# Modulation loads issued by SP, twelve weight low parts made on GpSimd, and four loads moved behind the stream

## The chip, the cores and the metric

The kernel runs on one core of one Trainium2 chip. The metric is the device time of one execution in microseconds, the median of several runs.

## The reference

Two transformer blocks in float32 on x of 1024 tokens by 1024 features, one after the other:

```
first_block:  x += hgrn2_mixer(rms(x)) ;  x += relu(rms(x) @ w1)^2 @ w2 ;  x = rms(x) * norm_final
second_block: sh1, sc1, g1, sh2, sc2, g2 = silu(c) @ w_ada + b_ada       (the same for the context, from c_ctx)
              hc = rms(ctx) * norm1 * (1 + csc1) + csh1                  (256 context tokens)
              hx = rms(x) * norm1 * (1 + sc1) + sh1
              kc, vc = hc @ w_in ;  fx, q, k, v = hx @ w_in
              y_four = real(fft2(fx)) ;  y_attn = windowed attention over k, v and kc, vc
              x += g1 * ((gate_f * (y_four @ w_fo) + gate_a * (y_attn @ w_ao)) @ w_o)
              x += g2 * relu((rms(x) * norm2 * (1 + sc2) + sh2) @ w1)^2 @ w2
```

Both hidden layers of the MLPs have 4096 features. silu(c) @ w_ada is a "modulation": 48 tiles for c and the first 16 of them for the context, each a product of a 128 x 1024 tile with a row, summed along the row.

## The kernel before, in words

**Precision.** Each float32 product is made of three TensorE products of rounded parts: `hi*hi`, `lo*hi`, `hi*lo`. ScalarE makes a high part (`Whi`, `Ah`, `Bh`, `ftr_h`, `wgt_h`, `Hh`) by a copy that rounds, VectorE the low part (`Wlo`, `Al`, ...) by a subtraction. Some low parts are made on GpSimd.

**Programs.** The five engines each run a program written by hand, one function for each (`tensor_program`, `sync_program`, `scalar_program`, `vector_program`, `gpsimd_program`). Each waits on semaphores by name, and its order is the order in the text. SP issues nearly all DMAs and stands when a DMA's condition isn't met; everything behind it in its program stands too.

**Weights.** Apart from those of the MLPs, weights come as a list `WT` of 128 x 1024 tiles of 512 KB. SP loads tile n into `Wraw[n % 2]` when tile n-2 has both its parts; ScalarE makes `Whi[n % 4]` and VectorE `Wlo[n % 4]` (line 1999) when TensorE has done with tile n-4. Every engine calls `feed(to)` at points in its program to go on to that tile. `S2_0[0]` is the number of the first tile of the second block. The tiles from there are, two each: ctx_v0, ctx_v1, ctx_k0, ctx_k1, u0, u1; then four of the Fourier matrix (dft), then others.

**An MLP** (`mlp(0)` and `mlp(1)`; the second is that of the second block) is done by a fast block scheme with seven products x = 1..7 of sums and differences of blocks.
- *Product stage*: 112 products s of 12 matmuls. They go through `SEQ`, by groups q of seven: 1, 5, then 4 of group q-1, 6, then 3 of q-1, 2, 7. For each group SP loads `pair_raw[q % 2]` (two DMAs of 512 KB, `pair_load`). VectorE makes sums of its pieces (`a_sum`, lines 2188 to 2200) four products ahead and low parts `Al` (`a_part`, line 2208) three ahead. VectorE scales and adds the results (`quarter`), ScalarE squares them, VectorE makes four sums of them (`feature_sums`), and SP writes three quarters and four sums of each group to `b_scratch` (256 KB each, at most three under way; `quarter_out`, `sums_out`).
- *Stream stage*: 56 steps g of 24 matmuls, 8 for each x in the order 1, 5, 6, 2, 7, 3, 4. SP's `step_load(j, g)` brings weights (`wgt_r`, for x = 5 and 7 also `other`) and features (`ftr_r`) when TensorE has done with the step that had the place (six before) and ScalarE is done with step g-4. `step_split` makes the four parts. In `mlp(0)` the last three steps of x = 4 go feature tile by feature tile (line 932).

**The modulations** are done on VectorE beside `mlp(0)`: `modulation(u)`, u = 0..97. It multiplies a 128 x 1024 tile `mraw` with `cvec` (line 2328) or, for u from 66 on, a tile of the second MLP's weights with the shift row (line 2332), and sums along it. u = 0 and u = 49 make the silu of `c` and `c_ctx` in `cvec`. Up to u = 48 they stand in the product stage, at every second product. The others stand in the stream by the table `MODS`: one in steps 4 to 7, 16, 17, 26 and on, two in steps 18 to 25. GpSimd's program issues the load of u (`mraw`, two buffers) as soon as modulation u-2 is done.

**Around the stream's end.** The final norm of the first block adds up squares in `facc`, on ScalarE (`final_square`), VectorE and GpSimd (`final_add`, lines 2341 and 2753), in steps 37 to 55. The context's squares are added in steps 41 to 43. In steps 49 and 53 ScalarE and VectorE call `feed` for the first four tiles, SP does at 44 and 51:

```
for g in range(7, 56):
    ...
    step_load(j, g)
    if j == 0:
        if g in (44, 51):
            sp.wait_ge(S("w_sum").at(39))
            feed(S2_0[0] + (2 if g == 44 else 4))
```

The tiles' places lie in memory that the stream's `wgt_s` and `other` hold until late. After the stream come: the root of the context norm, the context operand (`hcT`, `hch`, `hcl`), the last four final squares, the roots of the final norm for each half of the tokens, `HT` = the normed x of the second block (line 2440), `Hh` on ScalarE (line 1724), `Hl` on VectorE (line 2445). TensorE does ctx_v0, a sum, ctx_v1, ctx_k0, ctx_k1, then `u0` and `u1` from `Hh` and `Hl`, then dft.

Of the kernel before, what the change touches and what calls it, by code (L numbers as in the profile page):

```python
# [91 lines left out]
def build(nc, xT, vecs, w_in, w_out, m_w1, m_w2, ctxT, c_d, w_ada, w_in2, gains, biasE, biasM, w_gate, w_fo, w_ao,  # L92
          w_o2, m2_w1, m2_w1T, m2_w2, ident_d, masks_d, rope_d, dft_d, cd_d, out):
    with ExitStack() as ctx:
# [162 lines left out]
        S2_0 = [len(WT)]  # L257
        for c0 in (1536, 1792, 1024, 1280, 0, 256):
            WT += [cols256(w_in2, c0, 0), cols256(w_in2, c0, 512)]
        WT += [dft_d[par, cs].rearrange("(k p) c -> p k c", p=P) for par in range(2) for cs in range(2)]  # L260
# [49 lines left out]
        S = Sems()  # L310
# [197 lines left out]


        def tensor_program(pe):  # L510
# [19 lines left out]
            def lo_of(n):  # L530
                return S("w_lo", "v").at(n)
# [641 lines left out]
        def sync_program(sp):  # L1173
# [88 lines left out]
            def stream_loads(j):  # L1262
# [9 lines left out]
                if j == 0:  # L1272
                    e.dma_start(gnq[:], gains).then_inc(*S("gains").tick(0, 16))
                for g in range(7, 56):
# [7 lines left out]
                    if j == 0:  # L1282
                        if g in (44, 51):
                            sp.wait_ge(S("w_sum").at(39))
                            feed(S2_0[0] + (2 if g == 44 else 4))
                        if g == 24:
                            e.dma_start(cx[:], ctxT.rearrange("k p t -> p k t")).then_inc(*S("cx").tick(0, 16))
                    elif g in (42, 50):
                        result_out(2 if g == 42 else 7)
                if j:  # L1290
                    result_out(3)
                    result_out(4)

# [7 lines left out]
            def first_stage(j):  # L1301
# [102 lines left out]
        def scalar_program(act):  # L1404
# [322 lines left out]
            for g in range(4, 56):  # L1727
# [8 lines left out]
                if g in (49, 53):  # L1736
                    feed(S2_0[0] + (2 if g == 49 else 4))
# [6 lines left out]

            rstd("ctx_norm", 4, crs, 256)
# [243 lines left out]
        def vector_program(dve):  # L1989
# [3 lines left out]
            def feed(to):  # L1993
                for n in range(fed[0], to):
                    dve.wait_ge(S("w_hi").at(n))
# [347 lines left out]
            def beside(g):  # L2343
# [8 lines left out]
                if g in (49, 53):  # L2352
                    feed(S2_0[0] + (2 if g == 49 else 4))
# [93 lines left out]

            dve.wait_ge(stream_full(0, 52))
# [11 lines left out]
            for k in range(8):  # L2460
                h2_normed(k, 1)
                if k == 4:
                    feed(upto(("ctx_v0", 1)))
            mean_square(0)
            both_roots(0)
            feed(upto(("ctx_v1", 1)))
            for k in range(10):
                if k < 8:
                    h2_normed(k, 0)
                if k >= 2:  # L2470
                    h2_lo(k - 2)
                if k == 8:
                    feed(upto(("ctx_k0", 1)))
            feed(upto(("ctx_k1", 1)))
# [210 lines left out]
        def gpsimd_program(pool):  # L2685
            e = pool.e

# [43 lines left out]
            def modulation(u):  # L2731

                w, j = (0, u - 1) if u < 49 else (1, u - 50)
                if j < 0:
                    pool.wait_ge(S("ada").at(u - 1) if u else full_at(("mlp_norm", 0), 1))
                    e.dma_start(cvec[:], c_d[w]).then_inc(*S("c").tick(w, 16))
                    return
                if u in (1, 2):
                    pool.wait_ge(S("xs_out").at(0), S("lo", "v").at(b_lo(0, 3, 3)))
                elif u in (50, 51):  # L2740
                    pool.wait_ge(S("c_scaled").at(63))
                if u % 49 >= 2:
                    pool.wait_ge(S("ada").at(u - 2))
                e.dma_start(mod_place(u)[:], w_ada[j] if u < 66 else m2_w1T[u - 66]).then_inc(
                    *S("ada_raw", u % 2).tick(u, 16))

# [8 lines left out]
            for u in range(52):  # L2755
                modulation(u)
            for g in range(4, 56):
                for u in MODS.get(g, ()):
                    if u >= 52:
                        modulation(u)  # L2760
                if FINAL_AT.get(g, 11) not in (0, 4, 11):
                    final_add(FINAL_AT[g])
                for k in CTX_AT.get(g, ()):
                    if not 1 <= k < 7:
                        continue
                    pool.wait_ge(sq_of(4).at((4, k, 0, 0)))
                    if k > 1:
                        pool.wait_ge(sum_of(4).at((4, k - 1)))
                    e.tensor_tensor(cacc[:], cacc[:], csq[:], ALU.add).then_inc(*sum_of(4).tick((4, k)))
# [121 lines left out]
```

## Time and profile before

| | |
|---|---|
| median of 3 runs | 2678.27 us (2677.73 to 2681.16) |
| the profiled execution | 2677.73 us, its span 2675.9 us |
| TensorE (PE) busy | 2593.2 us, 97% of the span |
| VectorE (DVE) | 1743.1 us, 65% |
| ScalarE (ACT) | 1180.9 us, 44% |
| GpSimd (POOL) | 208.1 us, 8% |
| product stage of mlp(0) | about 600 to 928 us |
| stream stage of mlp(0) | about 928 to 1253 us |

The span goes from the first to the last instruction. Engines overlap, so their shares don't add up. In timelines and groups a row names line, engine, operation and output<-input; what stands in square brackets is how long the engine had been idle before it and what released it. SPq and POOLq are the issues of DMAs. A matmul's busy time overlaps its neighbours', so the distance of their starts is what one takes.

### The profile page before, as it was taken

To read this page: it belongs to the slowest core of one execution; us is meant where nothing else is said; L and a number is where in the kernel's file an instruction comes from. 1 tells how busy PE (TensorE), PEld (TensorE's weight loads), DVE (VectorE), ACT (ScalarE), POOL (GpSimd) and SP (SyncE) were. 2 spreads that over 40 slices of the span, in tenths; PEclk is the share of its full clock that TensorE was granted. 3 is DMA by queue.
4 is the path that set the end of the run, shared out by engine and by line. 5 is a ranking of instruction groups with operands and counts; after the bars stand their busy time and mean duration, and the time that the engine had idled before them with its cause. 6 is when DMAs were issued, how large, how long until landed. Compare 5 with 4: busy or idle time off the path is not lost.

```text
span 2675.9 us, 41694 instructions
## 1 busy us (share of the span) xinstructions
PE 2593.2 (97%) x16880; PEld 2162.6 (81%) x16880; DVE 1743.1 (65%) x2471; ACT 1180.9 (44%) x1852; POOL 208.1 (8%) x245
## 2 busy tenths in 40 slices
PE   8999999899999999999899999999899999999999
PEld 7887878687777787787889878977777888888887
DVE  6445454568888877897634565566566777768573
ACT  5454453544343443356333344244444555554341
POOL 2222122300000001132000000000000000000000
PEclk9999999999999999999999999999999999999999
DMA  4101111234776899983423212121352354488664
GB/s 138 41 25 48 36 30 41 80 110 154 235 230 215 282 375 328 338 294 127 145 85 120 69 57 78 33 70 57 132 207 95 121 167 139 164 313 290 236 224 140
DMA packets 289744, 406.12 MB, mean 152 GB/s; under 512 B 14736, under 2 KB 161680, under 8 KB 289552
## 3 DMA queue, kind: packets, MB, share of 16 engines
q1 hardware_dynamic: 275440, 352.07, 38.8%
q0 software_dynamic: 14112, 51.39, 5.7%
q8 instruction: 134, 2.20, 0.3%
q14 instruction: 58, 0.48, 0.1%
HBM read 314.27 MB, written 89.13 MB: 151 GB/s over the span
## 4 chain that ended last, share of the span: by engine, by line
PE 55%; DVE 12%; DMA 8%; issue 3%; ACT 3%; SPq 1%; DVEq 0%; ACTq 0%
PE ps L917 13%; PE ps L845 4%; PE ps L847 4%; PE ps L849 4%; DMA b_scratch<-qb 3%; PE ps L1101 2%; PE ps L1102 2%; PE ps L1106 2%; PE ps L567 2%; PE ps L551 2%; PE ps L554 2%; PE ps L635 2%; PE ps L633 2%; PE ps L637 2%; DVE Al L2208 1%
## 5 line engine op out<-in xcount | busy, mean ns | idle before, releaser
L847 PE MATMUL ps<-Bh,Al 128*128 128x512 f32 x896 | 352.4, 393 | 15.5 <-DVE Al L2208 15.5
L845 PE MATMUL ps<-Bh,Ah 128*128 128x512 f32 x896 | 351.5, 392 | 5.3 <-ACT wb L1598 3.9
L1999 DVE TENSOR_TENSOR Wlo<-Wraw,Whi 128x1024 fp32r<-128x1024 f32 x100 | 123.1, 1245 | 246.7 <-ACT Whi L1420 246.6
L849 PE MATMUL ps<-Bl,Ah 128*128 128x512 f32 x640 | 249.3, 389 | 0.0
L633 PE MATMUL ps<-Whi,Hh 128*128 128x256 f32 x768 | 222.4, 290 | 5.1 <-issue 5.1
L1620 ACT ACTIVATE ftr_h<-ftr_r 128x1024 fp32r<-128x1024 f32 x112 | 118.5, 1058 | 240.3 <-DMA ftr_r<-b_scratch 240.3
L635 PE MATMUL ps<-Wlo,Hh 128*128 128x256 f32 x768 | 217.9, 284 | 1.2 <-DVE Wlo L1999 1.2
L637 PE MATMUL ps<-Whi,Hl 128*128 128x256 f32 x768 | 217.6, 283 | 0.0
L917 PE MATMUL ps<-ftr_l,wgt_h 128*128 128x512 f32 x848 | 210.0, 390 | 5.3 <-DVE ftr_l L2276 5.3
L847 PEld LDWEIGHTS ps<-Bh,Al 128*128 128x128 f32 x896 | 169.2, 189 | 56.3 <-DVE Al L2208 21.1
L917 PE MATMUL ps<-ftr_h,wgt_h 128*128 128x512 f32 x848 | 210.1, 390 | 0.0
L917 PE MATMUL ps<-ftr_h,wgt_l 128*128 128x512 f32 x848 | 209.6, 389 | 0.0
L845 PEld LDWEIGHTS ps<-Bh,Ah 128*128 128x128 f32 x896 | 169.3, 189 | 42.8 <-ACT wb L1598 4.7
L1420 ACT ACTIVATE Whi<-Wraw 128x1024 fp32r<-128x1024 f32 x100 | 103.6, 1053 | 227.1 <-PE ps L567 92.0
L917 PEld LDWEIGHTS ps<-ftr_l,wgt_h 128*128 128x128 f32 x848 | 158.8, 188 | 39.8 <-DVE ftr_l L2276 6.9
L917 PEld LDWEIGHTS ps<-ftr_h,wgt_h 128*128 128x128 f32 x848 | 159.2, 188 | 33.5 <-issue 0.5
L917 PEld LDWEIGHTS ps<-ftr_h,wgt_l 128*128 128x128 f32 x848 | 159.1, 188 | 33.3 <-DVE wgt_l L2282 0.3
L2276 DVE TENSOR_TENSOR ftr_l<-ftr_r,ftr_h 128x1024 fp32r<-128x1024 f32 x112 | 136.9, 1222 | 28.3 <-ACT ftr_h L1620 28.2
L633 PEld LDWEIGHTS ps<-Whi,Hh 128*128 128x128 f32 x768 | 147.6, 192 | 7.1 <-issue 5.6
L635 PEld LDWEIGHTS ps<-Wlo,Hh 128*128 128x128 f32 x768 | 147.7, 192 | 1.6 <-DVE Wlo L1999 1.5
L637 PEld LDWEIGHTS ps<-Whi,Hl 128*128 128x128 f32 x768 | 147.7, 192 | 0.0
L849 PEld LDWEIGHTS ps<-Bl,Ah 128*128 128x128 f32 x640 | 120.3, 188 | 25.0
(372 smaller groups left out, 5471.0 us busy)
## 6 DMA issues: line engine op xcount, KB each, us to landing
b_scratch<-qb SPq DMA_DIRECT2D x224, 256.0 KB, 4.4
wgt_r<-in_m_w SPq DMA_DIRECT2D x112, 512.0 KB, 4.9
ftr_r<-b_scratch SPq DMA_DIRECT2D x112, 512.0 KB, 6.2
pair<-in_m_w SPq DMA_DIRECT2D x64, 512.0 KB, 5.3
mraw<-in_w_ada POOLq DMA_DIRECT2D x64, 512.0 KB, 5.5
Wraw<-in_w_in SPq DMA_DIRECT2D x56, 512.0 KB, 4.1
other<-in_m_w SPq DMA_DIRECT2D x32, 512.0 KB, 6.0
mraw<-in_m_w1T POOLq DMA_DIRECT2D x32, 512.0 KB, 5.4
```

What stands on the lines that cost most here:

```text
L551: e.matmul(t[:, c], wh[:, k, ms], opd.hi[:, k, c], start=k == 0, stop=False)
L633: e.matmul(o, opd.hi[:, k, c], wh[:, k % 4, :], start=k == 0, stop=False)
L635: e.matmul(o, opd.hi[:, k, c], wl[:, k % 4, :], start=False, stop=False)
L637: i = e.matmul(o, opd.lo[:, k, c], wh[:, k % 4, :], start=False, stop=k == 7)
L845: e.matmul(o, h[:, k, :], Bh[x][:, k, :], start=first and k == 0, stop=False, skip_group_check=not first)
L847: e.matmul(o, l[:, k, :], Bh[x][:, k, :], start=False, stop=False, skip_group_check=not first)
L849: i = e.matmul(o, h[:, k, :], Bl[x][:, k, :], start=False, stop=k == 3, skip_group_check=not first)
L917: ins = e.matmul(o(m), a, b, start=not cont and g == 8 * i and n == 0 and k == 0, stop=last, skip_group_check=cont)
L1420: e.activation(Whi[n % 4][:], Wraw[n % 2][:], ACT.Copy).then_inc(*S("w_hi").tick(n))
L1620: e.activation(ftr_h[p][:], ftr_r[p][:], ACT.Copy).then_inc(*S("a_hi").tick(2 * G))
L1999: e.tensor_tensor(Wlo[n % 4][:], Wraw[n % 2][:], Whi[n % 4][:].bitcast(F), ALU.subtract).then_inc(*S("w_lo", "v").tick(n))
L2276: e.tensor_tensor(ftr_l[p][:], ftr_r[p][:], ftr_h[p][:].bitcast(F), ALU.subtract).then_inc(*S("a_lo").tick(2 * G))
```

## The change

- SP's program issues the loads of the modulations; they leave GpSimd's program. In the product stage they stand behind products 6, 8, 9 and then every odd one. In the stream, u = 49, 50 and 51 stand in front of step 7's load, and those of `MODS[g - 1]` behind the load of step g.
- The load of a `pair` stands one product later in SP's program, behind the sums and a quarter of the product before: at product 4 of group q for group q+2. Before, it stood in front of them, at product 5.
- The first four tiles of the second block are no longer fed within the stream, on SP, ScalarE or VectorE, but behind it.
- `Wlo` of twelve tiles, from the fifth on (ctx_k0, ctx_k1, u0, u1, dft), is made by GpSimd. VectorE's `feed` skips them, and its calls for them in between `HT` and `Hl` go. TensorE and SP wait on GpSimd's semaphore for them.
- GpSimd's additions keep their order, without the loads between them.

```diff
+        LO_POOL = [len(WT) + 4, 0]
         for c0 in (1536, 1792, 1024, 1280, 0, 256):
             WT += [cols256(w_in2, c0, 0), cols256(w_in2, c0, 512)]
+        LO_POOL[1] = len(WT) + 4
...
         sync_program, feed:
-                        sp.wait_ge(S("w_hi").at(n - 2), S("w_lo", "v").at(n - 2))
+                        sp.wait_ge(S("w_hi").at(n - 2), S("w_lo", "p" if on_pool(n - 2) else "v").at(n - 2))
...
         stream_loads:
                 if j == 0:
+                    for u in (49, 50, 51):
+                        modulation(u)
                     e.dma_start(gnq[:], gains).then_inc(*S("gains").tick(0, 16))
                 for g in range(7, 56):
                     ...
                     step_load(j, g)
                     if j == 0:
-                        if g in (44, 51):
-                            sp.wait_ge(S("w_sum").at(39))
-                            feed(S2_0[0] + (2 if g == 44 else 4))
+                        for u in MODS.get(g - 1, ()):
+                            if u >= 52:
+                                modulation(u)
...
         first_stage:
-                    if x == 5 and 1 <= q % 16 < 15:
-                        pair_load(q + 1)
+                    if x == 4 and q % 16 < 14:
+                        pair_load(q + 2)
                     if s % NS >= 3:
                         if SEQ[s - 3][0] == 2 and SEQ[s - 3][1] % 16:
                             sums_out(SEQ[s - 3][1] - 1)
                         quarter_out(s - 3)
                     if s % NS in (107, 108, 111):
                         step_load(j, (107, 108, 111).index(s % NS))
+                    if s in (6, 8, 9):
+                        modulation((6, 8, 9).index(s))
+                    elif s < NS and s >= 11 and s % 2 and (s - 5) // 2 < 49:
+                        modulation((s - 5) // 2)
                 stream_loads(j)
             first_stage(0)
+            sp.wait_ge(S("w_sum").at(39))
+            feed(S2_0[0] + 2)
...
         scalar_program and vector_program, in the steps:
-                if g in (49, 53):
-                    feed(S2_0[0] + (2 if g == 49 else 4))
         behind the steps, ahead of the context root and norm:
+            feed(S2_0[0] + 4)
...
         vector_program:
             for k in range(8):
                 h2_normed(k, 1)
-                if k == 4:
-                    feed(upto(("ctx_v0", 1)))
             mean_square(0)
             both_roots(0)
-            feed(upto(("ctx_v1", 1)))
             for k in range(10):
                 if k < 8:
                     h2_normed(k, 0)
                 if k >= 2:
                     h2_lo(k - 2)
-                if k == 8:
-                    feed(upto(("ctx_k0", 1)))
-            feed(upto(("ctx_k1", 1)))
...
         gpsimd_program:
+            def feed(to):
+                for n in range(fed[0], to):
+                    if not on_pool(n):
+                        continue
+                    pool.wait_ge(S("w_hi").at(n), weight_full(n - 4))
+                    e.tensor_tensor(Wlo[n % 4][:], Wraw[n % 2][:], Whi[n % 4][:].bitcast(F), ALU.subtract).then_inc(
+                        *S("w_lo", "p").tick(n))
+                fed[0] = max(fed[0], to)
...
             norm_lo(HC, hcT, True, 256)
             for n in range(12, 15):
                 final_add(n)
+            for name in ("ctx_v0", "ctx_v1", "ctx_k0", "ctx_k1", "u0", "u1"):
+                feed(upto((name, 1)))
             pool.wait_ge(S("xs").at(7))
```

The function `modulation` of the GpSimd program goes to SP's as it is, its waits too: the load of u waits for modulation u-2.

## Rows read from the trace of the kernel before

**Rows 1.** TensorE's waits, whole span: us in total, times, longest.

```profile
PE ps L847 <- DVE Al L2208: 15.5, 11, 2.6
...
PE ps L917 <- DVE ftr_l L2276: 5.3, 3, 2.5
```

**Rows 2.** VectorE's waits in the product stage, 600 to 920.

```profile
DVE Xs L2188 <- DMA pair<-in_m_w: 34.8, 14, 4.5
```

**Rows 3.** VectorE's waits in the stream stage, 930 to 1240.

```profile
DVE mraw L2332 <- DMA mraw<-in_m_w1T: 10.2, 4, 2.9
DVE mraw L2328 <- DMA mraw<-in_w_ada: 8.3, 6, 2.0
```

**Rows 4.** Windows: busy us (instructions) of each engine, clock, DMA share, GB/s.

```profile
928.00:1000.00 72.00, 72.00 (x316) 58.91 (x315) 53.69 (x62) 31.98 (x32) 2.63 (x5) 1.00 1.01 374
1000.00:1100.00 100.00, 94.70 (x415) 77.39 (x414) 80.31 (x97) 33.68 (x33) 11.62 (x22) 1.00 0.93 329
1100.00:1150.00 50.00, 50.00 (x222) 41.40 (x221) 48.70 (x60) 21.23 (x23) 8.98 (x11) 1.00 0.98 361
...
1990.00:2676.00 686.00, 679.72 (x2982) 560.43 (x2981) 465.85 (x589) 318.58 (x448) 0.00 (x0) 1.00 0.55 186
```

**Rows 5.** Timeline of SP's queue: start, us, engine, line, what.

```profile
945.74 0.51 SPq L1273 DMA_DIRECT2D gnq<-in_gains  x1
...
1189.63 0.37 SPq L1256 DMA_DIRECT2D wgt_r<-in_m_w  x1
...
1205.75 1.50 SPq L1182 DMA_DIRECT2D Wraw<-in_w_in  x2
1207.35 0.64 SPq L1256 DMA_DIRECT2D wgt_r<-in_m_w  x1
```

**Rows 6.** Timeline of VectorE, 1180 to 1420.

```profile
1204.46 2.35 DVE L1999 TENSOR_TENSOR Wlo<-Wraw,Whi 128x1024 fp32r<-128x1024 f32 x2
...
1217.54 1.22 DVE L2276 TENSOR_TENSOR ftr_l<-ftr_r,ftr_h 128x1024 fp32r<-128x1024 f32 x1 [1.50 <-ACT ftr_h L1620]
...
1225.07 3.32 DVE L1999 TENSOR_TENSOR Wlo<-Wraw,Whi 128x1024 fp32r<-128x1024 f32 x2
...
1231.19 1.77 DVE L2341 TENSOR_TENSOR facc<-facc,ftmp 128x512 f32<-128x512 f32 x1
...
1254.40 3.95 DVE L2440 SCALAR_TENSOR_TENSOR HT<-R,modA,rs 128x512 f32<-128x512 f32 x5
1260.32 2.36 DVE L1999 TENSOR_TENSOR Wlo<-Wraw,Whi 128x1024 fp32r<-128x1024 f32 x2 [1.97 <-ACT Whi L1420]
```

**Rows 7.** Timeline of TensorE around the start of ctx_v0 and of u0.

```profile
1253.21 0.28 PE L633 MATMUL ps<-Whi,hch 128*128 128x256 f32 x1
1253.33 0.28 PE L635 MATMUL ps<-Wlo,hch 128*128 128x256 f32 x1
...
1284.95 0.55 PE L633 MATMUL ps<-Whi,Hh 128*128 128x256 f32 x1 [5.12 <-issue]
1286.73 0.58 PE L635 MATMUL ps<-Wlo,Hh 128*128 128x256 f32 x1 [1.23 <-DVE Wlo L1999]
```

**Rows 8.** Timeline of ScalarE, 1180 to 1420.

```profile
1234.31 1.28 ACT L1412 ACT_TABLE_LOAD   x1
```

**Rows 9.** The page's costliest groups: busy, mean ns, idle before.

```profile
L1999 DVE TENSOR_TENSOR Wlo<-Wraw,Whi 128x1024 fp32r<-128x1024 f32 x100 | 123.1, 1245 | 246.7 <-ACT Whi L1420 246.6
...
L1420 ACT ACTIVATE Whi<-Wraw 128x1024 fp32r<-128x1024 f32 x100 | 103.6, 1053 | 227.1 <-PE ps L567 92.0
```

**Rows 10.** DMA issues: count, KB each, median us to landing.

```profile
mraw<-in_w_ada POOLq DMA_DIRECT2D x64, 512.0 KB, 5.5
Wraw<-in_w_in SPq DMA_DIRECT2D x56, 512.0 KB, 4.1
```

**Rows 11.** GpSimd by shape, whole span; then its timeline.

```profile
L2727 POOL TENSOR_TENSOR Hl<-R,Hh 128x1024 fp32r<-128x1024 f32 x4 | 10.0, 2492 | 21.6 <-ACT Hh L1564 21.6
...
1224.17 2.01 POOL L2753 TENSOR_TENSOR facc<-facc,ftmp 128x512 f32<-128x512 f32 x1 [3.11 <-ACT ftmp L1699]
```

More of the change, by code:

```diff
@@ L507, in upto, with on_pool @@
             return min(WN[name] + 5, len(WT))
+        def on_pool(n):
+            return LO_POOL[0] <= n < LO_POOL[1]
         def tensor_program(pe):
@@ L530, in lo_of @@
             def lo_of(n):
-                return S("w_lo", "v").at(n)
+                return S("w_lo", "p" if LO_POOL[0] <= n < LO_POOL[1] else "v").at(n)
             def empty(b, occ):
@@ L1292, in stream_loads, with modulation @@
                     result_out(4)
+            def modulation(u):
+                w, j = (0, u - 1) if u < 49 else (1, u - 50)
+                if j < 0:
+                    sp.wait_ge(S("ada").at(u - 1) if u else full_at(("mlp_norm", 0), 1))
+                    e.dma_start(cvec[:], c_d[w]).then_inc(*S("c").tick(w, 16))
+                    return
+                if u in (1, 2):
+                    sp.wait_ge(S("xs_out").at(0), S("lo", "v").at(b_lo(0, 3, 3)))
+                elif u in (50, 51):
+                    sp.wait_ge(S("c_scaled").at(63))
+                if u % 49 >= 2:
+                    sp.wait_ge(S("ada").at(u - 2))
+                e.dma_start(mod_place(u)[:], w_ada[j] if u < 66 else m2_w1T[u - 66]).then_inc(
+                    *S("ada_raw", u % 2).tick(u, 16))
             def result_out(x):
@@ L1994, in feed @@
                 for n in range(fed[0], to):
+                    if on_pool(n):
+                        continue
                     dve.wait_ge(S("w_hi").at(n))
@@ L2351, in beside @@
                     modulation(u)
-                if g in (49, 53):
-                    feed(S2_0[0] + (2 if g == 49 else 4))
                 if g == 30:
@@ L2446, in h2_lo @@
                                        ALU.subtract).then_inc(*S("lo", "v").tick((5, k, 0)))
+            feed(S2_0[0] + 4)
             dve.wait_ge(stream_full(0, 52))
@@ L2686, in gpsimd_program @@
             e = pool.e
+            fed = [0]
+            def feed(to):
+                for n in range(fed[0], to):
+                    if not on_pool(n):
+                        continue
+                    pool.wait_ge(S("w_hi").at(n), weight_full(n - 4))
+                    e.tensor_tensor(Wlo[n % 4][:], Wraw[n % 2][:], Whi[n % 4][:].bitcast(F), ALU.subtract).then_inc(
+                        *S("w_lo", "p").tick(n))
+                fed[0] = max(fed[0], to)
             def norm_lo(opd, Tk, shifted=False, n=T):
@@ L2728, in gpsimd_program @@
                         *S("lo", "p").tick((2, h, 0)))
[L2731 to L2745, printed above, removed]
             def final_add(n):
@@ L2753, in final_add @@
                 e.tensor_tensor(to, to, ftmp[1][:], ALU.add).then_inc(*sum_of(5, 1).tick((5, n)))
[L2755 to L2769, printed above, removed]
+            for n in range(1, 4):
+                final_add(n)
+            for k in range(1, 7):
+                pool.wait_ge(sq_of(4).at((4, k, 0, 0)))
+                if k > 1:
+                    pool.wait_ge(sum_of(4).at((4, k - 1)))
+                e.tensor_tensor(cacc[:], cacc[:], csq[:], ALU.add).then_inc(*sum_of(4).tick((4, k)))
+            for n in range(5, 11):
+                final_add(n)
             norm_lo(HC, hcT, True, 256)
```

## The prediction

> **What bounds the kernel now.** I read the page first, then the windows of the stretch that the edits touch, then who waited for whom on TensorE and VectorE there, and last the timelines of SP, VectorE, ScalarE and GpSimd around the end of the first MLP. TensorE is the engine that sets the time nearly everywhere, so an edit counts only where it changes one of TensorE's waits. Of those waits the edits can reach five places. (a) In the product stage of the first MLP (about 600 to 928 us) TensorE waited 15.5 us for VectorE's low parts of the weight pieces [rows 1]; VectorE itself waited there 34.8 us, 14 times, for the `pair` loads [rows 2]. (b) In the stream stage it waited 5.3 us for `ftr_l` [rows 1]. VectorE was late there because it waited 18.5 us (10.2 + 8.3, ten waits) for the `mraw` loads of the modulations [rows 3], while the DMA engines were 0.93 to 1.01 occupied [rows 4]. (c) The last four steps of the stream: SP issued step 51's load at 1189.63, then stood before the `Wraw` loads until 1205.75, and the load of step 52 went out only at 1207.35 [rows 5]. (d) After the stream everything up to the `u0` product hangs on a chain of small steps on ScalarE and VectorE: last `facc` addition, root of the context norm, context operand, final norm, `HT`, `Hh`, `Hl`. TensorE began ctx_v0 at 1253.21, right behind its last stream product, `HT` began at 1254.40, and `u0` started at 1284.95 with 5.12 us of idle time and then stood 1.23 us more for `Wlo` [rows 6, 7]. (e) After `u0` has started, TensorE runs through `u0` and `u1`, 2 x 192 products of 0.12 us each [rows 7], for some 46 us, so that whatever is late by a few microseconds there is covered.
>
> **The change part by part.**
>
> *Loads of step 52 and on.* SP no longer stands for two `Wraw` buffers at step 51, so the loads of 52 to 55 go out as their places come free. VectorE loses from its queue ahead of the last `facc` addition: the two `Wlo` at 1204.46 (2.35 us), the 1.50 us wait for `ftr_h` at 1217.54, and the two `Wlo` at 1225.07 (3.32 us, one of them stretched) [rows 6]. That is 7.2 us. In the trace the last addition ended at 1231.19 + 1.77 = 1232.96.
>
> *The first four weights after the stream.* They now come after the last step on ScalarE and VectorE, in front of the context root. Before, the table load of that root began 1.35 us after the last addition (1234.31 [rows 8] minus 1232.96). In the new order a chain lies between: first `Whi` (1.05), first `Wlo` (1.25), the load of the third weight, which SP issues only when both are done (4.1 us to landing), the fourth about one `Wlo` later (1.2), its `Whi` (1.05) [rows 9, 10]. That adds 8.65 us. Together with the part before: 8.65 - 7.2 = +1.45 us for `HT`, if VectorE reaches step 51 when it does now.
>
> *VectorE's lead over TensorE.* The modulation loads move from GpSimd to SP. The 98 issues (64 + 32 of matrices, two of `cvec`) cost SP about 0.4 us each at most places where it waits anyway. What changes is order: a modulation's load now stands ahead of the next step's load in SP's queue, instead of sharing the DMA engines with it. The stretch with two modulations in a step is where VectorE waited. Between 1000 and 1150 the DMA engines were free for 7 us + 1 us [rows 4], and the bytes don't change, so I let VectorE get back 8 us of its 18.5 by that and 2 us by the better order: 10 us. Against it stands the switch to the second condition. Before, GpSimd fetched `cvec` long ahead. Now SP does so after the last sums, at the time of the gains' load (945.74 [rows 5]), and then waits for `cvec` to land, for its sigmoid and its multiplication, before it may load modulation 51 and then step 7: about 8 us of standing (5.5 for a 512 KB load [rows 10], 2.3 for two operations like those of [rows 9]). The DMA engines were full after 928 (1.01), so this isn't caught up at once; I charge 2 us of VectorE's lead. I expect no TensorE wait of it: from 928 to 1000 TensorE was busy all 72 us [rows 4], so the steps were ahead of it. Lead gained: 8 us, bounds 0 and 18.5. With it TensorE's 5.3 us of (b) vanish too, and the waits in the last steps, but they are no term: the chain of (d) is later than TensorE and decides. So `HT` starts 8 - 1.45 = 6.55 us earlier.
>
> *Twelve `Wlo` on GpSimd.* One took 1.25 us on VectorE [rows 9]; the nearest GpSimd row, the same operation on a 128x1024 tile, took 2.49 [rows 11]. GpSimd and VectorE also get in each other's way: beside the GpSimd addition at 1224.17 two VectorE subtractions took 3.32 us, where two by themselves took 2.35 [rows 11, 6]. What VectorE gains: it no longer stands for `Whi` and makes `Wlo` amid `HT` (1.97 idle + 2.36 at 1260.32 [rows 6], and the same twice more before `u0`), about 10 us, of which the chain gets some 3, since ScalarE's own order (`Whi`, copies, roots) holds the rest. What it costs: the weights 6 and 7 fall into the time of the `Hl` operations, one GpSimd operation in front of them, 2.4 us less what was in front anyway (1.5 to 2.5); `u0`'s first `Wlo` comes 1.25 us later after its `Whi` and the second one 2.5 us later, while TensorE wants it 12 products (1.4 us) after the first. I take +1 us from the start of `HT` to `u0` under way, bounds -2 (only the gain) and +9 (four operations at 2.4 on the chain). The last eight lie under `u0`, `u1` and the Fourier products: nothing.
>
> The Trainium skill has a rule against this part: SBUF — State Buffer, on the shared port pair, says that the lock is exclusive and the loser blocks for the whole instruction. The stretched subtractions, 1.0 us longer, agree as far as they go. By the rule alone all twelve would cost VectorE 12 x 2.4 = 29 us; the rows let only the four in the chain count.
>
> *The `pair` load one product later, behind the sums.* The load waits for its buffer, which VectorE frees at the second low part after; at SP's new place that condition is due at the same moment. The four sums and a quarter now go out before it. They are ready two products ahead, some 6 us (112 products fill the 328 us), three may be under way, and each is 256 KB, about 0.7 us at 374 GB/s [rows 4]. So nothing should be in front: 0 us, bounds -4 (the sums no longer behind 1 MB of `pair`) and +19 (two of them still under way, 1.3 us on each of 14 waits [rows 2]; there is no slack, as TensorE already waits). The same edit also stands in the second MLP, which has no modulations: there TensorE was busy 679.7 of 686 us [rows 4], so that nothing can be gained, and I expect nothing lost.
>
> **The sum.** 8.65 - 7.2 - 8 + 1 + 0 = -5.55 us. The profiled execution took 2677.73 us (span 2675.9), 0.5 less than the median of the three runs, 2678.27. Against the median: 2672.7.
>
> **The rivals.** *VectorE gains no lead (0.24).* Its modulations stay as late, because the DMA engines are full, or because SP's loads of the steps now wait for VectorE's modulations. Then +1.45 + 1, and up to +4 when `Wlo` on GpSimd costs more: 2679 to 2682. For it: 0.93 to 1.01 occupied [rows 4]. Against it: VectorE's ten waits are a latency chain of one buffer pair, not of bytes.
>
> A rule of the Trainium skill stands behind this rival: DMA: Bandwidth & Descriptors, in the section on queues, rings and completion order, says that a DMA engine goes round between its queues and takes one queue in ring order. By it a modulation in its own queue gets its share at once, and in SP's queue waits for all that was issued before. Its result would be that of this rival, about 2680; no row here separates the two orders.
>
> *More than I take (0.16).* VectorE gets back 15 us or more and the `HT` chain gains from the freed VectorE: 12 us less, 2666. It ends where TensorE's own stream end is the bound.
>
> *Slower: the `pair` loads come late (0.13).* Place: product stage of the first MLP. If the sums' writes or a modulation's load are still in SP's queue when the buffer comes free, each group of seven products gets longer by that time. At 0.7 us it costs 10 us, at 1.3 us 19 us; with the other terms 2683 to 2692. It decides from 0.8 us per group on (14 x 0.8 = 11, less 5.5, is +0.2%).
>
> *The change doesn't do what it says (0.05):* the late four loads are early, but the chain (d) is bound by ScalarE as before and everything cancels: 2677 to 2679.
>
> **How the numbers follow.** The forecast case, -2 to -8 us with the sum at -5.5, has 0.42: its own range is 2670 to 2676. What a measurement of this kernel can tell from no change is about 0.2%, 5.4 us, so that the forecast lies at the edge. Half of its chance and the whole of the larger gain are faster: 0.21 + 0.16 = 0.37. Slower: the `pair` case where it is past 0.8 us, 0.10, and the tail of the no-lead case in which `Wlo` on GpSimd costs all that its bound allows, 0.06: 0.16. The rest, 0.47, is no difference. For 8 in 10 the range reaches from 2666 (the larger gain) to 2684 (the no-lead case and the mild end of the `pair` case).
>
> **What would show it.** In the changed kernel: loads of steps 52 to 55 issued one by one from about 1193 us on, with no TensorE idle time at the `L932` group; VectorE's waits for `mraw` in the stream down from 18.5 to under 10 us; the table load of the context root about 6 us earlier; POOL operations of about 2.4 us for `Wlo`; `u0` about 5.5 us earlier, with the wait for `Wlo` 1 to 3 us; the product stage's waits for `Al` between 12 and 18 us. Wrong I would be if `Al` waits grow past 25 us, if `mraw` waits stay at 18, or if `u0` starts later though `HT` starts earlier.

## The result: slower by 1.05%

The changed kernel took 2706.30 us in the median (4 runs, 2704.74 to 2711.24), beside 2678.62 for the kernel before: a ratio of 1.0105, interval 1.0088 to 1.0122, that is 27.7 us more. The prediction was 2672.7 (2666 to 2684). It had the sign wrong, and the time lies outside the range. The profiled span went from 2675.9 to 2703.3, +27.4 us. Stage by stage, in one profiled execution of each, read from the starts of TensorE's and the other engines' rows:

| us | before | changed | difference | predicted |
|---|---|---|---|---|
| product stage, first MLP | 333.6 | 355.3 | +21.7 | 0 |
| stream start to the last `facc` addition ahead of the context root | 304.2 | 299.8 | -4.4 | -7.2 - 8 |
| from it to the root's table load | 1.4 | 10.5 | +9.1 | +8.65 |
| table load to the first `HT` | 20.1 | 20.1 | 0 | 0 |
| first `HT` to first `u0` product | 30.6 | 30.4 | -0.2 | } +1 |
| `u0` to the first Fourier product | 53.3 | 56.5 | +3.2 | } |
| product stage, second MLP | 312.9 | 311.0 | -1.9 | 0 |

TensorE's waits from 590 to 1370 us of the changed kernel (us in total, times, longest), against [rows 1]:

```profile
PE ps L852 <- DVE Al L2239: 29.6, 23, 2.6
...
PE ps L872 <- DVE facc L2372: 5.0, 1, 5.0
PE ps L640 <- POOL Wlo L2718: 4.8, 2, 3.5
...
PE ps L922 <- DVE ftr_l L2307: 1.9, 4, 0.9
```

The waits for `Al` doubled, from 11 to 23 and from 15.5 to 29.6 us, 14.1 of the 21.7 us. Most of the rest is matmuls that follow each other more slowly: TensorE was busy 321.9 us in this stage instead of 315.7, for the same 1354 recorded matmuls and at a granted clock of 0.99 in both. The waits for `ftr_l` shrank from 5.3 to 1.9, but TensorE now waited 5.0 us for `facc` and 4.8 for `Wlo`, where it was 1.2 for `Wlo` [rows 7].

VectorE's waits in the changed kernel: product stage (600 to 945; first row), then stream stage (950 to 1253), against [rows 2, 3]:

```profile
DVE Xs L2219 <- DMA pair<-in_m_w: 56.5, 14, 5.6
...
DVE wgt_s L2292 <- DMA ftr_r<-b_scratch: 13.4, 5, 6.9
DVE mraw L2363 <- DMA mraw<-in_m_w1T: 7.8, 5, 4.5
DVE cvec L2353 <- ACT mraw L1665: 6.3, 1, 6.3
DVE wgt_r L2297 <- DMA ftr_r<-b_scratch: 5.5, 5, 2.8
DVE wgt_s L2295 <- DMA ftr_r<-b_scratch: 5.5, 6, 1.7
DVE mraw L2359 <- DMA mraw<-in_w_ada: 1.6, 2, 0.9
DVE ftr_l L2307 <- ACT ftr_h L1650: 0.4, 1, 0.4
```

In the kernel before these rows of the stream (929 to 1236) stood beside those of [rows 3]:

```profile
DVE wgt_s L2261 <- DMA ftr_r<-b_scratch: 17.6, 6, 9.2
...
DVE ftr_l L2276 <- ACT ftr_h L1620: 2.1, 2, 1.5
DVE wgt_r L2266 <- DMA ftr_r<-b_scratch: 1.2, 1, 1.2
DVE wgt_s L2264 <- DMA ftr_r<-b_scratch: 1.0, 2, 0.5
```

Two things are to be seen. The waits for `pair` grew by 21.7 us, as much as the stage. And in the stream the `mraw` waits did fall, from 18.5 to 9.4 us, much as forecast; but all seven rows add up to 40.5 us, and the six of the kernel before to 40.4. The waits only changed their names: what VectorE no longer stood for `mraw` it stood for `cvec` and the steps' own loads.

**Where the pair is late.** SP's queue in the changed kernel, and VectorE beside it (start us, us, engine, line, what). The row at 696.14 holds two loads, the second of them issued at 705.07, and the row at 705.49 the four sums and a quarter:

```profile
696.14 9.25 SPq L1314 DMA_DIRECT2D mraw<-in_w_ada  x2
705.49 5.37 SPq L1236 DMA_DIRECT2D b_scratch<-qb  x5
710.98 1.14 SPq L1221 DMA_DIRECT2D pair<-in_m_w  x2
```

```profile
701.09 0.69 DVE L2276 TENSOR_TENSOR qb<-qb,qb 128x512 f32<-128x512 f32 x1
701.82 0.69 DVE L2278 TENSOR_TENSOR qb<-qb,qb 128x512 f32<-128x512 f32 x1
702.43 0.68 DVE L2279 TENSOR_TENSOR qb<-qb,qb 128x512 f32<-128x512 f32 x1
703.14 0.69 DVE L2281 TENSOR_TENSOR qb<-qb,qb 128x512 f32<-128x512 f32 x1
703.76 1.28 DVE L2359 CUSTOM_DVE_ANT_0 mraw<-mraw,cvec,vec 128x1024 f32<-128x1024 f32 x1
...
706.88 0.68 DVE L2239 TENSOR_TENSOR Al<-pair,Ah 128x512 fp32r<-128x512 f32 x1
```

The first of the four sums is ready at 701.8, and the pair's buffer is free at 707.57, when `Al` at 706.88 ends. But SP stands before a modulation's load, whose buffer VectorE frees with its modulation at 703.76, right behind the sums. SP goes on at 705.07, sends three sums by 706.9, waits until 709.8 for the first of them to land, sends the fourth and a quarter, and issues the pair at 710.98: 3.41 us late. A group has seven products and a modulation's load stands behind every second product, so in every second group a load comes right in front of the sums, behind product 1; in the other groups it comes behind them. Over the fourteen loads of `pair`, issue minus free buffer was 0.07 to 0.08 us in eight groups and 3.14 to 3.41 in six. Before, it was 0.07 to 0.09 in all fourteen. Six times 3.3 is 20 us.

**Around the stream's end.** VectorE, ScalarE and GpSimd of the changed kernel, three timelines:

```profile
1248.42 1.78 DVE L2372 TENSOR_TENSOR facc<-facc,ftmp 128x512 f32<-128x512 f32 x1
...
1252.52 2.36 DVE L2030 TENSOR_TENSOR Wlo<-Wraw,Whi 128x1024 fp32r<-128x1024 f32 x2
1258.21 1.23 DVE L2030 TENSOR_TENSOR Wlo<-Wraw,Whi 128x1024 fp32r<-128x1024 f32 x1 [3.33 <-ACT Whi L1450]
...
1280.81 10.17 DVE L2469 SCALAR_TENSOR_TENSOR HT<-R,modA,rs 128x512 f32<-128x512 f32 x8
...
1299.11 2.84 DVE L2469 SCALAR_TENSOR_TENSOR HT<-R,modA,rs 128x512 f32<-128x512 f32 x1
...
1303.07 0.74 DVE L2469 SCALAR_TENSOR_TENSOR HT<-R,modA,rs 128x512 f32<-128x512 f32 x1
```

```profile
1257.12 1.06 ACT L1450 ACTIVATE Whi<-Wraw 128x1024 fp32r<-128x1024 f32 x1 [3.68 <-DMA Wraw<-in_w_in]
1259.63 1.06 ACT L1450 ACTIVATE Whi<-Wraw 128x1024 fp32r<-128x1024 f32 x1 [1.45 <-DMA Wraw<-in_w_in]
1260.71 1.28 ACT L1442 ACT_TABLE_LOAD   x1
```

```profile
1285.18 5.24 POOL L2718 TENSOR_TENSOR Wlo<-Wraw,Whi 128x1024 fp32r<-128x1024 f32 x2 [3.65 <-ACT Whi L1450]
...
1311.17 6.34 POOL L2718 TENSOR_TENSOR Wlo<-Wraw,Whi 128x1024 fp32r<-128x1024 f32 x2 [9.76 <-ACT Whi L1450]
```

From the end of the last addition (1250.20) to the table load (1260.71) it is 10.51 us, where it was 1.35 [rows 6, 8]: the two reloads of `Wraw` stand in front of the root, 3.68 and 1.45 us of idle time on ScalarE. GpSimd took 2.6 to 3.2 us for a `Wlo` in the mean of these pairs, and VectorE's `HT` beside it took up to 2.89 us instead of 0.74.

### The profile page after: what moved, and what is told of

Same layout as the page of the kernel before. It is cut to its first block, busy times and chain, and to the rows that moved or that the text cites. A ratio compares the mean times of both kernels' runs of the same rounds, so it can differ in the third digit from the quotient of the medians.

```text
span 2703.3 us, 41694 instructions
## 1 busy us (share of the span) xinstructions
PE 2599.9 (96%) x16880; PEld 2163.4 (80%) x16880; DVE 1738.1 (64%) x2459; ACT 1180.8 (44%) x1852; POOL 188.6 (7%) x159
## 4 chain that ended last, share of the span: by engine, by line
PE 55%; DVE 12%; DMA 8%; ACT 4%; issue 3%; SPq 1%; POOL 0%; DVEq 0%; ACTq 0%
PE ps L922 13%; PE ps L850 4%; PE ps L852 4%; PE ps L854 4%; DMA pair<-in_m_w 3%; PE ps L556 2%; PE ps L572 2%; PE ps L559 2%; PE ps L1106 2%; PE ps L1107 2%; PE ps L1111 2%; DMA ftr_r<-b_scratch 2%; DMA b_scratch<-qb 2%; PE ps L640 2%; PE ps L638 2%
## 5 line engine op out<-in xcount | busy, mean ns | idle before, releaser
L852 PE MATMUL ps<-Bh,Al 128*128 128x512 f32 x896 | 353.6, 395 | 29.7 <-DVE Al L2239 29.6
L2030 DVE TENSOR_TENSOR Wlo<-Wraw,Whi 128x1024 fp32r<-128x1024 f32 x88 | 108.0, 1239 | 231.6 <-ACT Whi L1450 231.5
L852 PEld LDWEIGHTS ps<-Bh,Al 128*128 128x128 f32 x896 | 169.4, 189 | 75.4 <-DVE Al L2239 40.4
L2307 DVE TENSOR_TENSOR ftr_l<-ftr_r,ftr_h 128x1024 fp32r<-128x1024 f32 x112 | 138.2, 1234 | 27.8 <-ACT ftr_h L1650 27.7
L1617 ACT ACTIVATE Ah<-pair 128x512 fp32r<-128x512 f32 x160 | 98.1, 621 | 110.4 <-DMA pair<-in_m_w 77.6
```

Source lines behind the costliest of these rows:

```text
L852: e.matmul(o, l[:, k, :], Bh[x][:, k, :], start=False, stop=False, skip_group_check=not first)
L1617: e.activation(Ah[ring(s)][:], piece(x, q), ACT.Copy).then_inc(*S("a_part_hi").tick(s))
L2030: e.tensor_tensor(Wlo[n % 4][:], Wraw[n % 2][:], Whi[n % 4][:].bitcast(F), ALU.subtract).then_inc(*S("w_lo", "v").tick(n))
L2307: e.tensor_tensor(ftr_l[p][:], ftr_r[p][:], ftr_h[p][:].bitcast(F), ALU.subtract).then_inc(*S("a_lo").tick(2 * G))
```

## The experiments

Each is compared with the kernel before, run again on the same chip: its medians were 2680.4 to 2681.5 us there, with single executions from 2676.7 to 2687.8, so the ratios are to be compared and not the times. "Stage" is the first MLP's product stage, "head" the time from the stream's start to the last `facc` addition, "gap" from there to the table load (before: 333.6, 304.2, 1.4). Theory A through the study: SP's order delays the pair in six groups; rivals are the shared queue and the pair's place alone.

**e1: the pair's load back in front.**

```diff
 changed kernel, first_stage:
-                    if x == 4 and q % 16 < 14:
-                        pair_load(q + 2)
+                    if x == 5 and 1 <= q % 16 < 15:
+                        pair_load(q + 1)
```

> The changed kernel, with the load of a pair back in its old place, in front of the sums and the quarter. Theory A (order): in six of the fourteen groups the load of a pair is issued 3.3 us after its buffer is free, because SP reaches the four sums late (it stood for a modulation done by VectorE behind them), sends three at once, and holds the fourth until the first has landed. With the pair in front all fourteen are issued within 0.1 us: the product stage of the first MLP falls from 355.1 us by 19 to 21, the kernel by the same and up by 1.9 us in the second MLP: 2706.3 - 20 + 1.9 = about 2688. Rival B (share): the pair is late to land because the modulations' loads now stand in the same queue; then from issue to VectorE's start it stays above 6.6 us in the mean and the stage keeps over half of its excess: 2696 or more.

Measured 2736.19 us, ratio 1.0206 (1.0190 to 1.0221); stage 385.5 us. A's time was wrong by nearly 50 us. B's "2696 or more" holds in name only, since all but the first pair took 5.8 to 6.4 us from issue to VectorE's start, and B wanted over 6.6. The pairs were issued within 0.08 us of their buffers, but in this kernel's VectorE waits (600 to 930) another row had come on top:

```profile
DVE mraw L2359 <- DMA mraw<-in_w_ada: 51.1, 12, 6.0
DVE Xs L2219 <- DMA pair<-in_m_w: 22.0, 12, 2.9
```

SP now stands before the pair, and the modulations' loads behind it go out late; in its queue (same kernel) the pair ends a long stand, and the modulations follow behind six writes:

```profile
719.52 1.00 SPq L1221 DMA_DIRECT2D pair<-in_m_w  x2
720.62 7.61 SPq L1236 DMA_DIRECT2D b_scratch<-qb  x6
728.29 1.19 SPq L1314 DMA_DIRECT2D mraw<-in_w_ada  x2
```

So once the modulations are SP's, the pair's old place costs 30 us more than the new one. About 10 of the 30 are matmuls that follow each other more slowly: TensorE was busy 332.1 us in the stage at a granted clock of 0.96, instead of 321.9 at 0.99. The two edits can't be priced apart.

**e2: the pair's move alone.**

```diff
 kernel before, first_stage:
-                    if x == 5 and 1 <= q % 16 < 15:
-                        pair_load(q + 1)
+                    if x == 4 and q % 16 < 14:
+                        pair_load(q + 2)
```

> The kernel before, with nothing changed but the place of the load of a pair, one product later behind the sums and the quarter. Theory A: without a modulation ahead of them the sums are issued as soon as they are made, some 3.7 us before the pair's buffer is free, so the pair is issued at once: product stage of the first MLP 333 us +-1, the second MLP's 1.9 us shorter as in the changed kernel, 2678.6 - 1.9 = 2677. Rival C (the place alone costs it): the fourth sum's wait for a landing is 3 us in every group with or without modulations; then the pair is 1 to 3 us late in all fourteen groups and the kernel takes 2690 to 2700.

Measured 2683.22, ratio 1.0009 (1.0000 to 1.0019), all pairs within 0.09 us, stage 337.4. The place alone costs next to nothing, as A says, and C's 2690 is out of reach; A's own 333 us and 2677 were missed by 4 and 6 us (see the last section for how far the stage varies). The second MLP took 313.0 us, so the 1.9 us were no gain of the place: with the old place in e1 it took 311.0.

**e3: modulations 0 to 48 on GpSimd again.** SP's calls in `first_stage` go, GpSimd's program gets them (and semaphores of its own).

```diff
 changed kernel, sync_program, first_stage:
-                    if s in (6, 8, 9):
-                        modulation((6, 8, 9).index(s))
-                    elif s < NS and s >= 11 and s % 2 and (s - 5) // 2 < 49:
-                        modulation((s - 5) // 2)
 gpsimd_program:
+            for u in range(49):
+                modulation(u)
```

> The changed kernel, with the loads of the 49 modulations of the product stage issued by GpSimd again; those of the stream, the new place of the pair, the late weights and the low parts on GpSimd stay. Theory A: product stage back to 333 us +-1, kernel about 2706.3 - 21.7 = 2684.6. Rival C (the pair's new place alone is to blame): stage stays at 345 to 355, kernel 2696 to 2706.

Measured 2694.29, ratio 1.0046 (1.0030 to 1.0063), stage 340.7, pairs within 0.09 us. Over half of the loss is gone with this edit alone (ratio 1.0105 to 1.0046); but the stage lies 7 us above the expected 333 +-1 and the kernel 10 us above 2684.6. VectorE waited 40.2 us for the pairs, where it was 34.8 [rows 2], though all were issued in time (see the last section).

**e5: the wrong modulation moved.** The load behind product 7 went behind the next group's sums.

```diff
+                        if x == 5 and q and s >= 13:
+                            modulation((s - 7) // 2)
+                        if x != 7 or q == 15:
+                            modulation((s - 5) // 2)
```

> The changed kernel, with one SP order changed: the modulation load that stands behind a product 7 (every second group) goes behind the next group's four sums and quarter, still ahead of the pair at its new place, still issued by SP. Theory A (SP stood at that load while the sums were ready): the sums go out about 2 us earlier, the pair of those six groups is issued with 0 to 1.3 us delay instead of 3.3, and the stage shortens by 12 to 20 us: 2686 to 2694. Rival B (the queue is shared with the modulations) or C (the pair's place): the stage stays within 4 us of 355, kernel 2702 to 2707.

Measured 2713.61, ratio 1.0119 (1.0103 to 1.0134), stage 360.4, the same six pairs 3.2 to 3.4 us late. This seemed to speak for B or C, but the load had been misplaced: a product 7 with a modulation precedes the groups whose pairs are in time. In the late ones the load in front of the sums is that of product 1. The experiment tested nothing that it was meant to; e6 is the mended one.

**e6: the modulation behind product 1 goes behind the sums.** Still SP's, with the pair at its new place.

```diff
+                        if x != 1:
+                            modulation((s - 5) // 2)
+                    elif s < NS and s >= 12 and s % 2 == 0 and x == 5 and (s - 6) // 2 < 49:
+                        modulation((s - 6) // 2)
```

> The changed kernel, with one order in SP's program changed: where a modulation's load stands behind a product 1 (in every second group, those whose pair is late), it goes behind the four sums and the quarter of product 5, still ahead of the pair's load and still issued by SP. Theory A (SP stood there for a modulation that VectorE does right behind the sums): the sums go out as soon as they are made, all fourteen pairs are issued within 0.2 us of their buffer, the product stage of the first MLP takes 335 to 342 us instead of 355, and the kernel 2687 to 2693. Rival (late for another reason, as the three writes in flight alone): pairs stay over 2 us late in six groups and the kernel within 4 us of 2706.

Measured 2686.99, ratio 1.0026 (1.0015 to 1.0036); stage 335.7, all fourteen pairs within 0.09 us. Its queue shows the order, sums first, then the modulation, then the pair as soon as its buffer is free:

```profile
742.14 3.15 SPq L1236 DMA_DIRECT2D b_scratch<-qb  x5
745.40 0.39 SPq L1314 DMA_DIRECT2D mraw<-in_w_ada  x1
747.98 1.01 SPq L1221 DMA_DIRECT2D pair<-in_m_w  x2
```

One load, moved by one place in six groups, takes the ratio from 1.0105 to 1.0026, some 20 us. B falls with it: the modulations are in the same queue as in the changed kernel.

**e11: six writes under way instead of three.**

```diff
-                if v >= 3:
-                    sp.wait_ge(S("a_out", v % 3).at(v - 3))
+                if v >= 6:
+                    sp.wait_ge(S("a_out", v % 6).at(v - 6))
```

> The changed kernel, with up to six writes of features under way instead of three; SP's order stays. Theory A has two parts: in six groups SP comes to the sums late, 2.1 us before the pair is due, and then stands 3.4 us for the landing of the first of three. Without the second part five writes go out in about 2.2 us (0.44 each) and the pair is 0.1 to 0.5 us late instead of 3.3: stage 336 to 342 us, kernel 2687 to 2693. Rival (the late start decides, the landing doesn't): the pair stays 3 us late and the kernel at 2706.

Measured 2704.54, ratio 1.0083 (1.0070 to 1.0096), stage 355.0: nothing is won in the stage, and this part of A falls. (The ratio is 0.2% lower, but the two intervals overlap.) The pair was issued 1.3 to 1.5 us late instead of 3.3, but took 7.4 to 9.2 us from issue to VectorE's start instead of 6.0 to 7.2:

```profile
752.24 3.35 SPq L1236 DMA_DIRECT2D b_scratch<-qb  x5
755.68 1.55 SPq L1221 DMA_DIRECT2D pair<-in_m_w  x2
```

So 1.9 us of standing went and 1.5 us of landing came, in the means of the six groups. The reading is that the writes right ahead of the pair cost the same whether SP waits for their landing or the pair lands behind them; no run tests it further. With e6, what decides is when SP comes to the sums.

**e4: modulations 49 to 51 on GpSimd too.**

```diff
 e3, stream_loads:
-                    for u in (49, 50, 51):
-                        modulation(u)
```

> The changed kernel, with the loads of modulations 0 to 51 issued by GpSimd (those of the product stage and those around the switch to the second condition); 52 and on stay with SP. Theory A: SP no longer stands for the second condition before the load of step 7, so VectorE doesn't lose 6.1 us there; what was left of that loss at the end of the stream was 1.8 us, so the last addition before the context root comes 1.8 us earlier after the stream's start than in the run with 0 to 48 on GpSimd, and the kernel takes 2694.3 - 1.8 = 2692.5. Rival: the loss doesn't fade and 6 us come back: 2688. Rival: the loads in the stream by SP cost the lead by themselves: nothing comes back, 2694.

Measured 2686.48, ratio 1.0019 (1.0010 to 1.0028). Head 296.0 us, where e3 had 300.5: the switch costs 4.5 us at the stream's end, not 1.8, and the rival's 2688, by which the loss doesn't fade, came nearest. The 1.8 was probably what remained after a gain of the loads from 52 on had been set off against it.

**e7: the four weights behind the stream, alone** (in the kernel before; SP's, ScalarE's and VectorE's `feed` as in the change).

> The kernel before, with nothing changed but the first four weights of the second block: fed behind the stream on SP, ScalarE and VectorE, as in the changed kernel. Theory A: the last addition before the context root comes 6.2 us earlier, the chain of the four weights in front of the root costs 9.2 us: the first operation of HT 3.0 us later after the stream's start, kernel +3, a ratio of 1.001. Rival (what the prediction took, with the lead): -7.2 + 8.65, +1.5 us. Rival (the early loads gain what the modulations had hidden): 3 us or more faster.

Measured 2684.56, ratio 1.0017 (1.0008 to 1.0026). Head 298.4, gap 10.6: -5.8 and +9.2, `HT` 3.5 us later, as A has it. From there 2.2 us come back: the first `HT` to `u0` took 28.4 us instead of 30.6, because `Whi` was ready sooner for the `Wlo` amid `HT`. VectorE idled 0.41 us before the first two, where it was 1.97 [rows 6]:

```profile
1266.10 2.36 DVE L1998 TENSOR_TENSOR Wlo<-Wraw,Whi 128x1024 fp32r<-128x1024 f32 x2 [0.41 <-ACT Whi L1420]
```

What is left at the Fourier product is +1.9 us. The kernel is slower by 0.17%, clear of its interval; in the profiled execution 4.3 us of that stand in the product stage, which this edit doesn't touch.

**e8: the twelve low parts on GpSimd, alone.**

> The kernel before, with nothing changed but the low parts of the twelve weights, made on GpSimd. Theory A: one takes 2.4 us by itself and 2.6 to 3.2 beside VectorE, whose operations it stretches; from the start of HT to u0 0 to 1 us shorter (VectorE no longer makes eight of them, but 8 HT take 10 us instead of 5.3), the wait for the first Wlo of u0 3.5 us instead of 1.2, up to the Fourier product 1 us more: kernel +3 us. Rival (the gain of 10 us of VectorE's time gets through to the chain): -3 to -8 us. Rival (an exclusive lock for each operation, all twelve on the chain): +15 us or more.

Measured 2683.20, ratio 1.0010 (1.0002 to 1.0019). First `HT` to `u0` 30.2 us (30.6 before), `u0` to the Fourier product 55.8 (53.3): +2.1 us, near A. (In e2, whose code there is that of before, the same stretch was 0.8 us longer than before.) The gain of VectorE's time doesn't reach the chain. Beside GpSimd's `Wlo` of this kernel one `HT` took 2.89 us, the next ones 0.74:

```profile
1276.02 2.89 DVE L2447 SCALAR_TENSOR_TENSOR HT<-R,modA,rs 128x512 f32<-128x512 f32 x1
...
1280.03 0.74 DVE L2447 SCALAR_TENSOR_TENSOR HT<-R,modA,rs 128x512 f32<-128x512 f32 x1
```

**e9 and e10: two weights in front of the root, two behind the operand.** e9 is the kernel before with this (SP as in the change); e10 has also the loads of modulations 52 and on with SP.

```diff
 scalar_program (vector_program likewise, around hcT and hcl):
+            feed(S2_0[0] + 2)
             rstd("ctx_norm", 4, crs, 256)
             norm_hi(HC, hcT, mc(0, 1), 256)
+            feed(S2_0[0] + 4)
 e10, stream_loads, behind step_load(j, g):
+                        for u in MODS.get(g - 1, ()):
+                            if u >= 52:
+                                modulation(u)
```

> The kernel before, with the first four weights of the second block out of the stream, but only two of them in front of the context root; the other two are made behind the context operand. Theory A: the last addition 6 us earlier, as with all four behind; from it to the table load of the root 2 to 3 us instead of 10.6 (before: 1.4), since no reload is waited for; the other two cost 0 to 2.5 us between the operand and HT. First operation of HT 2 to 5 us earlier after the stream's start than before; kernel 0.1 to 0.2% faster. Rival: the two behind the operand cost as much there as in front: HT as before or later, ratio 1.000 to 1.002.

> The same, and the loads of modulations 52 and on issued by SP behind the step loads (0 to 51 stay with GpSimd, the pair's load stays in front, all low parts on VectorE). Theory A: SP's loads in the stream gave 2.4 us (298.4 to 296.0 from the stream's start to the last addition, with all other edits of the stream's end the same), so HT comes 2.4 us earlier than with the split alone: kernel 0.15 to 0.35% faster than before. Rival: that 2.4 us is variation of the stream; the same time as the split alone.

e9: 2680.97, ratio 0.9997 (0.9989 to 1.0006). Head 299.2, gap 3.3 as expected, but the other two cost 2.6 us behind the operand, so `HT` is only 0.5 us earlier: the rival was right. As in e7, the first `HT` to `u0` took 28.4 us, so that `u0` began 2.7 us earlier. e10: 2676.51, ratio 0.9981 (0.9973 to 0.9990), head 295.0, `HT` 4.6 us earlier. It is the only version here that beats the kernel before, by 0.19%, 5 us in the medians.

## Why the prediction was wrong

- **Pair load, "nothing should be in front: 0 us".** This step failed, and with it the forecast: the stage took 21.7 us more, 17 to 20 of them by this. I had the sums ready two products ahead, which is right (701.8 for 707.6), and asked only whether they would be slow once issued. I did not ask whether SP would be free to issue them. In six of fourteen groups it stood before a modulation's load whose condition VectorE meets only behind the sums. The rival "slower" named this place, and the whole stage loss of 21.7 us is a little past its upper price of 19 (14 x 1.3 is 18.2); but it had 1.3 us in fourteen groups, where it was 3.3 in six, so the closeness of the two sums is luck. e6 shows the cause. I gave it 0.13 because I counted the modulations' 98 issues at 0.4 us "at most places where it waits anyway", and not what stands behind each such wait. Its bound of -4, for sums no longer behind the pair, gave nothing either: in e2 the writes did land sooner, and the stage took 337.4 us. DMA issues of the kernel before, then of e2:

```profile
b_scratch<-qb SPq DMA_DIRECT2D x224, 256.0 KB, 4.4
...
b_scratch<-qb SPq DMA_DIRECT2D x224, 256.0 KB, 2.1
```

- **VectorE's lead, -8 us.** It failed too: the head fell by 4.4 us in the changed kernel, and the late weights alone give 5.8 (e7), so instead of a lead of 8 us some 1.4 were lost, outside the bounds of 0 and 18.5. 10 us from the `mraw` waits: they fell by 9.1, but the loads of steps 52 and on by SP gave the head only 2.4 us (e4 against e7; 4.2 in e10 against e9). Kernels with the same code in the stream differ there by up to 3.1 us (before 304.2, e8 304.6, e2 301.5), so the size is uncertain. VectorE waited for other loads instead; in a stage whose DMA engines are 0.93 to 1.01 occupied [rows 4] this is what the no-lead rival said. The switch to the second condition, charged at 2, cost 4.5 (e4). SP took `cvec`'s load and the two modulations at 965.94 to 972.69 in front of step 7's load, and VectorE stood 6.3 us for `cvec`.
- **Late loads and four `feed`s, -7.2.** 5.8 by e7. Right in kind, 1.4 us too large.
- **First four weights in front of the root, +8.65.** 9.1 in the changed kernel, 9.2 in e7. Right, with the two reloads as its main part.
- **Twelve `Wlo` on GpSimd, +1.** +2.1 in e8 and +3.0 in the changed kernel against the one before, from the first `HT` to the Fourier product. Against e7, which has the late weights too, it is +4.7 (86.9 us to 82.2): the two edits don't add up, since the 2.2 us that the late weights give back amid `HT` are lost again. All of it lies within the bounds of -2 and +9. The 10 us that VectorE was to gain counted three pairs of `Wlo` before `u0`; the third began at 1285.46, after `u0`, and without idle time. The Trainium skill's rule in SBUF — State Buffer, on the shared port pair (the loser blocks for the whole instruction), fits the 2.89 us `HT`. The 29 us that it would make of all twelve came to 2 to 5: TensorE waited for two of the twelve, 3.5 and 1.3 us, and for none of the last six.
- **Pair load in the second MLP, 0.** Right: 311.0 to 313.0 us in all kernels, with either place.

One of the prediction's own signs of being wrong came: the waits for `Al` grew to 29.6 us, past 25. And the table load of the context root came 4.8 us later after the stream's start, where it was to come 6 earlier. The sign for `mraw`, under 10 us, came true (9.4) and meant nothing by itself.

By single edits: the weights behind the stream, the low parts on GpSimd and the pair's move each cost 0.1 to 0.2% alone (the pair's move with an interval that begins at 1.0000); the modulations on SP in the stream gave 2 to 4 us, the switch took 4.5, and the product stage's modulations in front of the sums took 17 to 20.

## What to carry to other kernels

When an issue moves to a queue that stands on conditions, write down for each period of the loop which engine frees it, behind which of its operations, and which issues stand behind it; if loop and issues have different periods, do so for every phase of the beat. A wait that goes away is worth nothing until the sum of all waits of that engine in the stage has gone down. Order edits in one queue have no price of their own: the same move of `pair` cost 0.1% in one kernel and gained 30 us in the other.

## What was not expected

- **The product stage varies where its code is the same.** It took 333.6 us in the profiled execution of before and 337.9, 337.5, 337.1 and 340.8 in e7, e8, e9 and e10, whose code there is the same, with every pair issued in time. From issue to VectorE's start a pair took from 5.7 to 9.6 us in these five. Each trace is one execution, and single executions of the kernel before differ by 11 us (2676.7 to 2687.8), with the profiled one among the fastest; so this need not be a difference of the kernels. Some 4 or more of the 21.7 us may be such variation, and the six late loads explain 17 to 20. What sets the landing was not found.
- **A narrow VectorE operation beside a wide GpSimd one takes nearly four times as long:** `HT` 2.84 and 2.89 us for 0.74, on 128x512, beside a 128x1024 subtraction that GpSimd does in 2.4 us alone. GpSimd is stretched too: the two at 1311.17, the first of them beside `Hl`, took 6.34 us.
- **The modulations' loads landed sooner, and not because SP issued them.** From the DMA issues of the changed kernel, against [rows 10], and of e3, where GpSimd issues those of the product stage and the pair keeps its new place:

```profile
mraw<-in_w_ada SPq DMA_DIRECT2D x64, 512.0 KB, 4.1
...
mraw<-in_w_ada POOLq DMA_DIRECT2D x48, 512.0 KB, 4.1
```

  The median from issue to landing is 4.1 us in both, where it was 5.5 before. What goes with it is the pair's place: in e2, which moves nothing else, the 48 loads of the product stage have a median of 3.95 us from GpSimd's queue, the changed kernel's 4.01 from SP's, the kernel before's 4.89. The Trainium skill's rule that one queue is taken in ring order (DMA: Bandwidth & Descriptors, queues, rings and completion order) would have a load wait behind SP's others. That agrees with the pair in e11, 7.4 to 9.2 us behind five writes, but doesn't show in these medians.
